# A stationary operand stored with its high and low halves side by side, 2080 bytes a tile

## The reference

```python
h = rmsnorm(x, w);   proj = h @ w_in        # [256,2048] @ [2048,8192]
y = recurrence(proj), short_conv(proj)
x = x + concat(y) @ w_out                   # [256,2048] @ [2048,2048]
g, u = split(rmsnorm(x, w) @ w_gate_up)     # [256,2048] @ [2048,11264]
x = x + (silu(g) * u) @ w_down              # [256,5632] @ [5632,2048]
# second layer: a product with w_in_2, low-rank attention and stick-breaking attention,
# a gated merge, w_out_2, and again a gated feed-forward part; the norms are scaled and
# shifted by c @ w_ada_2, a product with a single row
```

## Time and profile before

| | |
|---|---|
| two timed runs | 2704.24 and 2706.6 us, median 2705.42 us |
| the profiled execution | 2706.13 us |
| its span, first to last instruction | 2704.1 us |
| outside the span | 2.0 us |
| TensorE matmul busy | 2664.6 us, 99% of the span |
| TensorE weight load busy (beside the matmuls) | 2213.9 us |
| VectorE busy | 1750.9 us, 65% |
| ScalarE busy | 1305.8 us, 48% |
| HBM read | 577.76 MB, 214 GB/s with what is written |
| granted TensorE clock, mean | 0.997 of full speed |

### The profile page before, as it was taken

How to read it: one execution, slowest core, us unless ns; L and a number is a source line. 1 busy time by engine, 2 the same in 40 slices (tenths; PEclk the granted TensorE clock), 3 DMA queues, 4 the chain that set the end, 5 groups by cost and what they waited for, 6 DMA issues and landing times.

```text
span 2704.1 us, 33965 instructions
## 1 busy us (share of the span) xinstructions
PE 2664.6 (99%) x12453; PEld 2213.9 (82%) x12453; DVE 1750.9 (65%) x2052; ACT 1305.8 (48%) x1546; POOL 3.2 (0%) x9
## 2 busy tenths in 40 slices
PE   8999999999999999999899999999899999999999
PEld 6888888878888888888787888888788888888887
DVE  5788677477676767788775554575576644445565
ACT  5555554354444444445555566644444444444443
POOL 0000000000000000000000000000000000000000
PEclk9999999999999999999999999999999999999999
DMA  7766554678788888888565455555578766665555
GB/s 253 246 205 188 154 150 152 221 242 283 272 281 274 279 273 288 291 282 268 169 205 170 140 165 170 178 182 179 177 250 282 241 191 187 193 186 173 197 191 171
DMA packets 302070, 581.43 MB, mean 215 GB/s; under 512 B 19934, under 2 KB 20280, under 8 KB 301704
## 3 DMA queue, kind: packets, MB, share of 16 engines
q1 hardware_dynamic: 300912, 576.34, 66.0%
q10 hardware_dynamic: 744, 2.27, 0.2%
q0 software_dynamic: 304, 1.33, 0.2%
HBM read 577.76 MB, written 2.10 MB: 214 GB/s over the span
## 4 chain that ended last, share of the span: by engine, by line
PE 93%; DVE 4%; ACT 2%; issue 1%; DMA 0%; SPq 0%; ACTq 0%; DVEq 0%
PE acc L346 29%; PE acc L348 29%; PE acc L347 29%; DVE lo L335 2%; PE ex L1018 1%; PE aux L1039 1%; PE tp L1407 1%; PE aux L575 1%; ACT hi L329 0%; PE tp L516 0%; DVE op_lo L487 0%; PE aux L2122 0%; ACT stage L479 0%; PE aux L2121 0%; DVE op_hi L486 0%
## 5 line engine op out<-in xcount | busy, mean ns | idle before, releaser
L335 DVE TENSOR_TENSOR lo<-raw,hi 128x1024 fp32r<-128x1024 f32 x895 | 1078.3, 1223 | 506.6 <-ACT hi L329 486.0
L329 ACT ACTIVATE hi<-raw 128x1024 fp32r<-128x1024 f32 x895 | 928.2, 1056 | 669.1 <-PE acc L348 538.4
L346 PE MATMUL acc<-hi,op_hi 128*128 128x512 f32 x2752 | 1088.1, 395 | 13.0 <-DVE lo L335 10.2
L348 PE MATMUL acc<-hi,op_lo 128*128 128x512 f32 x2752 | 1073.8, 390 | 0.0
L347 PE MATMUL acc<-lo,op_hi 128*128 128x512 f32 x2752 | 1072.8, 390 | 0.0
L346 PEld LDWEIGHTS acc<-hi,op_hi 128*128 128x128 f32 x2752 | 517.8, 188 | 125.6 <-issue 18.3
L348 PEld LDWEIGHTS acc<-hi,op_lo 128*128 128x128 f32 x2752 | 517.3, 188 | 109.9
L347 PEld LDWEIGHTS acc<-lo,op_hi 128*128 128x128 f32 x2752 | 518.1, 188 | 102.7 <-issue 0.2
L346 PE MATMUL acc<-hi,f_hi 128*128 128x512 f32 x704 | 275.3, 391 | 0.9 <-DVE lo L335 0.8
L561 DVE SCALAR_TENSOR_TENSOR ada_acc<-ada_ring,cact,ada_acc 128x512 f32<-128x512 f32 x360 | 269.7, 749 | 7.3 <-DVE h_a L898 0.3
L348 PE MATMUL acc<-hi,f_lo 128*128 128x512 f32 x704 | 274.0, 389 | 0.0
(11 more groups left out here) (315 smaller groups left out, 1420.4 us busy)
## 6 DMA issues: line engine op xcount, KB each, us to landing
raw<-w_in SPq DMA_DIRECT2D x257, 512.0 KB, 3.9
ada_ring<-w_ada SPq DMA_DIRECT2D x192, 512.0 KB, 5.1
raw<-w_gate_up SPq DMA_DIRECT2D x176, 512.0 KB, 4.9
raw<-w_ffn_in SPq DMA_DIRECT2D x176, 512.0 KB, 4.5
raw<-w_down SPq DMA_DIRECT2D x88, 512.0 KB, 5.7
raw<-w_ffn_out SPq DMA_DIRECT2D x88, 512.0 KB, 4.3
raw<-w_out SPq DMA_DIRECT2D x64, 512.0 KB, 4.5
raw<-w_proj_mla SPq DMA_DIRECT2D x16, 512.0 KB, 4.1
```

Source lines behind the costliest of these rows:

```text
L329: A.activation(hi[:, k, :, 0:n], raw[:, k, :, 0:n], ACT.Copy).then_inc(hi_ready, 1)
L335: V.tensor_tensor(lo[:, k, :, 0:n], raw[:, k, :, 0:n], hi[:, k, :, 0:n].bitcast(F32), ALU.subtract).then_inc(lo_ready, 1)
L346: T.matmul(dst, lh, hi[:, k, kk, 0:n], start=first and kk == 0, stop=False)
L348: mm = T.matmul(dst, ll, hi[:, k, kk, 0:n], start=False, stop=last and kk == CK - 1)
```

## The change

The two tensors become one, in which a tile's high half (256 values) and low half (256 values) follow each other, and eight values (32 bytes) stay unused behind them. The names `op_hi` and `op_lo` become views of it, so that every instruction, wait and loop stays as it is; only start addresses and the distance from tile to tile (now 2080 bytes instead of 1024) differ. The tensor takes 512 bytes of a partition more than the two did, and what is allocated behind it lies 512 bytes higher.

```diff
-        op_hi = sb("op_hi", [P, KT, S], F32R)
-        op_lo = sb("op_lo", [P, KT, S], F32R)
+        op = sb("op", [P, KT, 2 * S + 8], F32R)
+        op_hi, op_lo = op[:, :, 0:S], op[:, :, S:2 * S]
```

## The result

The changed kernel takes 2747.03 us (median of 2746.34 to 2747.73) against 2705.42 us: 41.6 us more, a ratio of 1.0154 with a 95% interval of 1.011 to 1.0197. The profiled execution has a span of 2744.3 us against 2704.1, 40.2 us more, at the same mean granted clock of 0.997.

The account below looks back on a forecast made before the run. The prediction took TensorE to bound the kernel, as a count of matmuls times the distance between starts. All terms summed to 0 us against the profiled 2706.1 us, giving 2706 us, range 2680 to 2750.

Parts of the forecast that it names:

- third rival: Matmul stream at `op` settles at another pace, between 0.224 and 0.232 us: 2684 to 2749 us, chance 0.10.
- What bounds the kernel: TensorE matmuls cover 99% of the span; time is a count of matmuls times the distance between starts.
- price of a load beside the stream: Loading 128 weight columns beside a running matmul adds some 13.3 ns to each distance between starts.
- Distance between high and low half: Weights' high-low distance falls from 16 KB to 1 KB; claimed to cost 0 us.
- Shift within 512 bytes: Tile starts shift 0 to 480 bytes; claimed 0 us, bounded by 109 us faster and 102 us slower.
- The range's bound from rows 9: Nine distances after an interruption averaged 0.232 us; 5 ns on 8160 matmuls would be 43 us slower, 22 us faster.
- The sign of the third rival: In the steady stream at `op`, a distance of 0.232 us or a pace differing from tile to tile.
- The 16-byte lines of the Trainium skill: A 512-byte weight load touches 32 SBUF lines before and after, 32 periods or 13.3 ns; so 0 us.
- Separate ports for weights and moving columns: The skill says loading takes no read bandwidth from the running matmul, 215.7 ns for 512 columns; the trace shows 227.
- The cast: VectorE cast at L486 keeps its rate despite writing two runs: 0 us, at most 13 us.
- The first two rivals: Load stops colliding: 2597 us, chance 0.10. Load at a shifted start costs more: 2808 us, chance 0.10.
- second rival: Shifted weight loads need more fetch pieces; half more tax shows as 2% slower, doubled gives 2808 us; chance 0.10.

Follow-up runs that it names:

- e3: Kernel before with `op_hi` and `op_lo` moved by a constant 32 bytes, the rest of memory kept on 512-byte places: 2753.6 us, ratio 1.0175.
- e1: Changed kernel without the 32 unused bytes, halves side by side at a tile pitch of 2048 bytes: 2706.73 us, ratio 0.9999 against the kernel before.
- e5: Kernel before with `op_hi` and `op_lo` moved by a constant 64 bytes, the rest kept on 512-byte places: 2754.24 us, ratio 1.0175.
- e8: Kernel before with `op_hi` and `op_lo` moved by a constant 480 bytes, 32 before a 512-byte place: 2753.66 us, ratio 1.0172.
- e12: Kernel before with `op_hi` and `op_lo` as views beginning 16 bytes inside one tensor, all else on 512-byte places: 2733.56 us, ratio 1.0097.
- e11: Kernel before with the rings `raw`, `hi` and `lo` moved by 32 bytes, everything from `op_hi` on left in place: 2768.01 us, ratio 1.0229.
- e4: Kernel before with everything from the raw buffers on moved by 32 bytes, relative places kept: 2705.47 us, ratio 0.9997.
- e10: Kernel before, asked for a 240-byte shift; the allocator's rounding gave 256 for `op` and 32 for all other weights: 2721.46 us, ratio 1.0056.
- e6: Kernel before with `op_hi` and `op_lo` moved by a constant 128 bytes, the rest kept on 512-byte places: 2747.3 us, ratio 1.0149.

## Why the prediction was right or wrong

The time, 2747 us, lies in the range of 2680 to 2750, and within 2% of before. The central forecast of 2706 us was wrong: there is a slowdown, well beyond the noise, and it is of the size of the third rival, which had a chance of 0.10. That the range holds it is luck. The time lies 3 us under the upper bound, whose reason fails below, and the same change with one constant shift of 32 bytes (e3, 2753.6 us) would have been outside.

**What bounds the kernel: right.** TensorE bounds it, and the only term with a sum in it was the price of a load beside the stream. The whole change came through that term, in the 8160 matmuls that were counted, and 5 ns on each of them is the 41 us.

**Distance between high and low half, 0 us: right,** by e1.

**Shift within 512 bytes, 0 us: the step that failed.** The argument was that two readers of unequal speed pass through the whole pattern during one load, so that the start could only change the order. e3, e5 and e8 refute it: the same shift in every load gives a steady price of 48 periods instead of 32. e12 refutes the second half by itself: with the same addresses the stream rests at 226.7 or at 233.3 ns, so the order in which the readers meet does set a price. Whether the slip fails already before that, in the pace of the load or in the assumption that the load keeps its pace beside a matmul, no run here shows. The prediction itself said that all rows of before agree in their place within 512 bytes and so can't exclude a rule there; it then gave that rule too small a chance.

**The range's bound from rows 9: near in size, wrong in its reason.** Nine unsettled distances at 0.232 us gave 43 us. The working is loose: 5 ns on 8160 matmuls is 41 us, and 2.09 / 9 less 0.2267 is 5.6 ns, 45 us. The changed kernel runs at 0.2326 us. But it is not that each new tile sets a stream off that would come to rest at the old pace: with one constant shift it rests at 0.2333 us, slower than with changing ones. The sign of the third rival, a pace that differs from tile to tile, did appear. In its long runs at `op` the changed kernel takes for the twelve matmuls of a chunk, two tiles, 2.785, 2.784, 2.798 and 2.800 us in turn and then the same again, a cycle of eight tiles or 256 bytes. At rest at 0.2267 us it would be 2.720, at 0.2333 us 2.800. So the chunks with a tile at shift 0 or 256 are only a little cheaper: the price of a tile depends on the tiles before it too.

**The 16-byte lines of the Trainium skill** ("SBUF — State Buffer", section "Door 1: The DMA port swizzle (why `[64,N]` ≈ `[32,N]`)"). The fit of 32 lines to 32 periods held for equal starts alone: e3 touches 32 whole lines as well and pays 48 periods. The count of lines touched doesn't set the price.

**Separate ports for weights and moving columns** (the Trainium skill, "TensorE: Matmul & The Clock Gate", section "Step-by-step: what each phase is for"). The prediction set this against the 227 ns of the trace and left open what addresses do. The runs here disagree with the part that a load takes nothing from the running matmul: moving one operand by 32 bytes relative to the other takes the distance from 0.2267 to 0.2333 us (e3 and e11), also where the other engines or the DMA are idle (e3). Whether the ports are separate, they don't show.

**The cast, 0 us: right,** at 427 ns. Its bound of 13 us wasn't needed.

**The first two rivals** didn't occur. No shift brought the price under 32 periods, and a boundary that the weights want for themselves is excluded by e4. The settled price did rise by one half, 32 to 48 periods, the size from which the second rival was to show as 2%; it came from the relative place and not from pieces, and it stays short of 2% because some matmuls of the kernel before weren't at rest (e3) and because the price of the changed kernel is less than that of a constant shift.

What stays open is the mechanism below that. The runs show how the price goes with the relative place, that 256 bytes count as 0, and the two rest paces; what in the memory or in TensorE makes it so, they don't show. Shifts of 96, 160 and 192 bytes, or under 16, were not run alone.

## What to carry to other kernels

In a kernel that streams 512-column matmuls, each with its own weight load, put the weights and the moving columns at the same place within 256 bytes; a gap of 32 bytes between tiles cost 1.5% here, while no gap, or a constant shift of 256 bytes, cost nothing. Watch the remainder that a small tensor leaves behind it, for it shifts all that follows (e10 lost 0.6% that way). When every row of a trace shares a property that the change takes away, a uniform pace in that trace is no evidence that the property doesn't matter.

## What the runs showed of the hardware

- A load of 128 float32 weights beside a 512-column matmul costs 13.3 ns (0.2267 us from start to start) when both start at the same place within 256 bytes, and 20 ns (0.2333 us) at 32, 64 or -32 bytes from it (e3, e5, e8). At 128 bytes it settles at 0.2324 or 0.2333 us (e6).
- It is the relative place that counts: all tensors from the rings on moved by 32 bytes together cost nothing (e4, 0.9997), the rings alone 2.3% (e11).
- At a shift of 16 bytes one program shows both paces, 0.2267 and 0.2333 us, each for 190 matmuls on end, and changes between them at interruptions alone (e12).
- The price does not come from other engines or from DMA: the distance at a shift of 32 bytes is 233.3 ns with ScalarE and VectorE idle and 233.3 with both at work, and 233.1 without any DMA packet under way (e3).
- A VectorE cast of 512 values takes 427 ns whether its destination is one run or two with a gap.
